# Second layer of a two-layer mixer on one core: keys projected in one load ahead of the last gate-input load, values in whole tiles behind the last queries, key norms earlier

## What is computed

```python
z = h @ o_w_in
c_u, c_v, cq, ckv, kr = split(z, [512, 1024, 1408, 1664])
yc = spatial_gating(gelu(c_u), gelu(c_v), w_s, bias, v_gain)
q  = (rmsnorm(cq) @ w_uq).reshape(s, 8, 96)
kv = (rmsnorm(ckv) @ w_ukv).reshape(s, 8, 128)
k_nope, v = kv[..., :64], kv[..., 64:]
q, k = rmsnorm per head and part, rope on 32 columns, shared rotary key joined to k_nope
yd = softmax(chunk-causal q k) v
y  = concat(rmsnorm(yc), rmsnorm(yd)) @ o_w_out
```

## Time and profile before

| | us |
|---|---|
| median of 3 runs (lowest, highest) | 1105.81 (1105.48, 1106.58) |
| the profiled execution, its own time | 1106.4 |
| its span, first to last instruction | 1104.6 |
| PE busy (matmuls) | 1096.0 (99%) |
| DVE busy | 548.3 (50%) |
| ACT busy | 418.3 (38%) |
| POOL busy | 104.4 (9%) |
| mean granted TensorE clock | 1.000 |

### The profile page before, as it was taken

One profiled execution on the slowest core, in us unless ns is written; L12 is line 12 of the kernel. 1 busy time (PEld: TensorE's weight loads), 2 busy tenths in 40 slices (PEclk: granted clock), 3 DMA queues, 4 the chain that ended last, 5 costly groups with the idle time before them and its releaser, 6 DMA issues. The chain is left out here.

```text
span 1104.6 us, 13734 instructions
## 1 busy us (share of the span) xinstructions
PE 1096.0 (99%) x5148; PEld 883.8 (80%) x5148; DVE 548.3 (50%) x770; ACT 418.3 (38%) x663; POOL 104.4 (9%) x126
## 2 busy tenths in 40 slices
PE   9999999999999999999999999999999999999998
PEld 7777788888888888888878766788888888888887
DVE  6677967344334433242466588655434433453321
ACT  5546435333223222131446557545223322332110
POOL 6000000010001000000102023000001100100000
PEclk9999999999999999999999999999999999999999
DMA  7522233332333333332233200233333233327431
GB/s 225 172 58 82 72 105 106 96 95 88 101 95 95 95 96 97 99 103 88 72 96 93 84 20 2 77 115 95 96 96 99 89 112 96 95 77 173 113 125 47
DMA packets 103241, 106.00 MB, mean 96 GB/s; under 512 B 26267, under 2 KB 79968, under 8 KB 103200
## 3 DMA queue, kind: packets, MB, share of 16 engines
q1 hardware_dynamic: 85488, 103.04, 30.6%
q10 hardware_dynamic: 16656, 2.10, 1.2%
q0 software_dynamic: 1056, 0.30, 0.1%
HBM read 101.23 MB, written 2.10 MB: 94 GB/s over the span
## 5 line engine op out<-in xcount | busy, mean ns | idle before, releaser
L1126 DVE TENSOR_TENSOR w_lo<-raw,w_hi 128x1024 fp32r<-128x1024 f32 (+2 forms) x192 | 224.6, 1176 | 420.7 <-ACT w_hi L700 417.9
L700 ACT ACTIVATE w_hi<-raw 128x1024 fp32r<-128x1024 f32 (+2 forms) x192 | 194.4, 1017 | 466.7 <-PE ps L1688 434.9
L1686 PE MATMUL ps<-h_hi,w_hi 128*128 128x512 f32 x912 | 359.7, 394 | 0.7 <-DVE h_lo L1150 0.7
L1687 PE MATMUL ps<-h_lo,w_hi 128*128 128x512 f32 x912 | 355.1, 389 | 0.0
L1688 PE MATMUL ps<-h_hi,w_lo 128*128 128x512 f32 x912 | 355.1, 389 | 0.0
L1686 PEld LDWEIGHTS ps<-h_hi,w_hi 128*128 128x128 f32 x912 | 171.3, 188 | 41.3 <-issue 5.6
L1687 PEld LDWEIGHTS ps<-h_lo,w_hi 128*128 128x128 f32 x912 | 171.3, 188 | 36.6 <-issue 1.7
L1688 PEld LDWEIGHTS ps<-h_hi,w_lo 128*128 128x128 f32 x912 | 171.2, 188 | 36.0
L584 POOL TENSOR_TENSOR ffn_t<-ffn_t,row_scale 128x512 f32<-128x512 f32 x40 | 50.9, 1294 | 606.9 <-ACT ffn_t L887 606.9
L1687 PE MATMUL ps<-w_lo,act_hi 128*128 128x512 f32 (+1 forms) x178 | 68.8, 387 | 0.0
L1688 PE MATMUL ps<-w_hi,act_lo 128*128 128x512 f32 (+1 forms) x178 | 68.8, 387 | 0.0
(11 more groups left out here) (288 smaller groups left out, 1151.7 us busy)
## 6 DMA issues: line engine op xcount, KB each, us to landing
raw<-in_w_ffn_in SPq DMA_DIRECT2D x88, 512.0 KB, 3.5
raw<-in_w_ffn_out SPq DMA_DIRECT2D x44, 512.0 KB, 3.9
raw<-in_e_w_in SPq DMA_DIRECT2D x17, 512.0 KB, 3.7
raw<-in_o_w_in SPq DMA_DIRECT2D x8, 512.0 KB, 3.6
raw<-in_o_w_out SPq DMA_DIRECT2D x8, 512.0 KB, 3.7
raw<-in_e_w_out SPq DMA_DIRECT2D x8, 256.0 KB, 3.9
raw<-in_e_w_out SPq DMA_DIRECT2D x4, 512.0 KB, 4.7
out_tok<-x_blocks ACTq DMA_DIRECT2D x16, 128.0 KB, 2.6
```

Source lines behind the costliest of these rows:

```text
L700: ins = act.activation(dst, src, ACT.Copy)
L1126: ins = TT(dst, src, high, ALU.subtract)
L1686: MM(dst, st_hi, mv_hi, start=start, stop=False)
L1687: MM(dst, st_hi, mv_lo, start=False, stop=False)
```

## The change

It renumbers the loads: 104, 105 queries, 106 to 108 c_u, 109 keys of all eight heads (`O_UK`), 110 last c_u load, 111, 112 queries, 113 values of all heads (`O_UV`). The loads 109 and 113 take 64 of every 128 columns of `w_ukv`, in two transfers each.

```diff
-O_CQ, O_CKV, O_CV, O_UKV, O_OUT = 92, 96, 100, 112, 114
-O_UQ, O_CU = (104, 105, 110, 111), (106, 107, 108, 109)
+O_CQ, O_CKV, O_CV, O_OUT = 92, 96, 100, 114
+O_UQ, O_CU, O_UK, O_UV = (104, 105, 111, 112), (106, 107, 108, 110), 109, 113
...
+            if n in (O_UK, O_UV):
+                free(n)
+                for k in range(2):
+                    sp.dma_start(raw[:, n % 2, 512 * k:512 * k + 512].rearrange("p (h c) -> p h c", h=HEADS),
+                                 w_ukv[:, k, :, 0 if n == O_UK else 1, :]).then_inc(raw_landed[n % 2], 16)
...
# ACT
         through(107)
+        through(108)
+        key_squares()
+        key_gains()
+        through(109)
+        rms(M_OK, ps[:, 4, :], 1)
         gelu_table()
-        through(109)
         for j in range(4):
             act.wait_ge(u_scaled, j + 1)
             act.activation(u_c[:, j, :], u_c[:, j, :], ACT.Gelu_apprx_tanh).then_inc(u_ready, 1)
-        q_squares(2, 4)
+        q_squares(2, 6)
         through(110)
         rms_table()
         q_squares(3, 6)
-        yc_square(0)
-        yc_square(1)
-        key_squares(0)
-        rms(M_OQ + 1, ps[:, 3, :], 1)
-        yc_square(2)
-        yc_square(3)
-        key_squares(1)
-        key_gains_1()
-        rms(M_OK, ps[:, 4, :], 1)
-        value_copy(0, 0, 0)
-        rms(M_OC, ps[:, 1, :], 512)
+        for j in range(4):
+            yc_square(j)
+        for t in range(QT):
+            value_copy(t)
+        rms(M_OQ_LATE, ps[:, 6, :], 1)
+        rms(M_OC, ps[:, 7, :], 512)
         exp_table()
...
# DVE
         through(108)
+        key_gains()
+        through(109)
         dve.wait_ge(load_used, O_CU[3] + 1)
         for j in range(4):
             TT(u_c[:, j, :], ps[:, j, :], row_scale[:, :], ALU.mult).then_inc(u_scaled, 1)
-        through(109)
-        q_tiles(2, 4)
+        rms(M_OK, ps[:, 4, :], 1)
         through(110)
+        q_tiles(2, 6)
+        k_norm(0)
+        k_norm(1)
...
-        yc_gate(0)
-        yc_gate(1)
+        for j in range(4):
+            yc_gate(j)
         q_tiles(3, 6)
-        yc_gate(2)
-        yc_gate(3)
-        key_gains_0()
-        rms(M_OQ + 1, ps[:, 3, :], 1)
-        yc_sum(1)
-        yc_sum(2)
-        q_scale(1, (0, 1, 2, 3))
-        rms(M_OK, ps[:, 4, :], 1)
-        yc_sum(3)
-        value_copy()
-        k_norm(0)
+        for j in range(1, 4):
+            yc_sum(j)
+        k_norm(2)
+        k_norm(3)
...
+        dve.wait_ge(ov_act, 3)
+        for i in range(QT):
+            set_mask(i)
+        rms(M_OQ_LATE, ps[:, 6, :], 1)
+        rms(M_OC, ps[:, 7, :], 512)
...
         o_max(0)
-        k_norm(2)
+        q_scale(1, (3, 6, 7, 4))
         o_prob(0)
         o_max(1)
         o_pt(0)
         o_prob(1)
         o_max(2)
-        k_norm(3)
...
# PE
         cu_load(2)
+        pe.wait_ge(ckv_lo_ready, 2)
+        pe.wait_ge(oq_scaled, 4)
+        load(O_UK, plain(512, 4), range(2), lambda k: (ckv_hi[:, k, :], ckv_lo[:, k, :]), range(4, 8), True, True)
         cu_load(3)
-        pe.wait_ge(oq_scaled, 2)
-        q_load(2, 4)
+        pe.wait_ge(ok_squared, 4)
+        pe.wait_ge(ok_gained_dve, 1)
+        sums4(4, [mean64[:, 48:80]] * 4, [q_sq(p) for p in range(4)])
+        pe.wait_ge(ok_gained, 2)
+        q_load(2, 6)
+        pe.wait_ge(ok_gained_dve, 2)
+        spread(M_OK, (4, 5))
         pe.wait_ge(u_scaled, 4)
         pe.wait_ge(cv_normed, 4)
...
-        pe.wait_ge(oq_scaled, 4)
+        pe.wait_ge(oq_turned, 6)
         q_load(3, 6)
...
+        ready(O_UV)
+        value_tile(0)
+        value_tile(1)
+        pe.wait_ge(ok_normed, 4)
+        spread(M_OK, (4, 5), 2)
+        value_tile(2)
+        value_tile(3)
+        q_sums(1, 6)
         pe.wait_ge(yc_summed, 4)
-        mean(M_OC, 1, ones, acc[:, :])
+        mean(M_OC, 7, ones, acc[:, :])
...
-                    pe.wait_ge(banks_set, (2, 5, 5, 5)[n])
+                    pe.wait_ge(banks_set, 4)
...
         o_scores(0)
-        pe.wait_ge(ov_act, 2)
-        value_tiles(1, 1, 3)
-        pe.wait_ge(ok_normed, 2)
+        pe.wait_ge(ov_act, 4)
+        pe.wait_ge(rs_step, M_OC + 1)
+        pe.wait_ge(ok_normed, 6)
+        spread(M_OQ_LATE, (3, 6, 7, 4))
         o_scores(1)
-        pe.wait_ge(ov_act, 3)
-        pe.wait_ge(ok_normed, 6)
+        pe.wait_ge(oq_scaled, 8)
+        pe.wait_ge(ok_normed, 8)
```

More of the change, by code:

```diff
@@ L101, in load_dmas @@
         return 3
+    if n in (O_UK, O_UV):
+        return 2
     return 1
@@ L507, in _ @@
             wide(O_CV + j, oin, 256 * j, 512, 512)
-        for n in range(O_UQ[0], O_UKV):
+        w_ukv = o_w_ukv[0].rearrange("(k p) (h two c) -> p k h two c", p=P, two=2, c=64)
+        for n in range(O_UQ[0], O_OUT):
             if n in O_CU:
                 wide(n, oin, 256 * O_CU.index(n), 0, 512)
+                continue
+            if n in (O_UK, O_UV):
+                free(n)
+                for k in range(2):
+                    sp.dma_start(raw[:, n % 2, 512 * k:512 * k + 512].rearrange("p (h c) -> p h c", h=HEADS),
+                                 w_ukv[:, k, :, 0 if n == O_UK else 1, :]).then_inc(raw_landed[n % 2], 16)
                 continue
@@ L712, in through, with spare_column @@
                 nxt[0] += 1
+        n_spare = [0]
+        def spare_column():
+            n_spare[0] += 1
+            return spare[:, n_spare[0] - 1:n_spare[0]]
         def exp_table():
-            act.activation(spare[:, :], eps_col[:, :], ACT.Exp)
+            act.activation(spare_column(), eps_col[:, :], ACT.Exp)
         def rms_table():
-            act.activation(spare[:, :], eps_col[:, :], ACT.Abs_reciprocal_sqrt)
+            act.activation(spare_column(), eps_col[:, :], ACT.Abs_reciprocal_sqrt)
         def h_high_first(ft):
@@ L980, in gelu_table, with key_squares, key_gains, value_copy @@
         def gelu_table():
[L982 to L996, removed]
-            else:
-                act.wait_ge(ov_tiles, half + 1)
-            act.activation(o_v[:, 2 * part:2 * part + 2, 256 * half:256 * half + 256],
-                           ps[:, bank, :].rearrange("p (t c) -> p t c", t=2), ACT.Copy).then_inc(ov_act, 1)
+            act.activation(spare_column(), eps_col[:, :], ACT.Gelu_apprx_tanh)
+        def key_squares():
+            act.wait_ge(load_used, O_UK + 1)
+            for p in range(4):
+                act.activation(q_sq(p), ps[:, 4 + p, :], ACT.Square).then_inc(ok_squared, 1)
+        def key_gains():
+            for p in (2, 3):
+                act.wait_ge(ok_squared, p + 1)
+                act.activation(k_pairs[:, p, :], ps[:, 4 + p, :], ACT.Copy, scale=g_col(G_OK)).then_inc(ok_gained, 1)
+        def value_copy(t):
+            if t == QT - 1:
+                act.wait_ge(load_used, O_UV + 1)
+            else:
+                act.wait_ge(ov_tiles, t + 1)
+            act.activation(o_v[:, t, :], ps[:, t, :], ACT.Copy).then_inc(ov_act, 1)
         def yc_square(j):
@@ L1725, in sums4, with spread @@
             ins.then_inc(sums_ready, 1)
-        def spread(m, banks):
+        def spread(m, banks, g0=0):
             pe.wait_ge(rs_ready, m + 1)
-            for g, b in enumerate(banks):
+            for g, b in enumerate(banks, g0):
                 ins = MM(ps[:, b, :], sel[32 * g:32 * g + 32, :], rs_of(m)[32 * g:32 * g + 32, :], start=True, stop=True)
@@ L2112, in value_tiles @@
[L2112 to L2137, removed]
@@ L2138, in _, with value_tile @@
-        spread(M_OK, (4, 5, 6, 7))
-        pe.wait_ge(oq_scaled, 6)
+        def value_tile(t):
+            pe.wait_ge(gates_ready, t + 1)
+            for kk in range(2):
+                c = slice(512 * kk, 512 * kk + 512)
+                ins = product(ps[:, t, :], ckv_hi[:, kk, t * P:(t + 1) * P], ckv_lo[:, kk, t * P:(t + 1) * P],
+                              w_hi[:, O_UV % W_SLOTS, c], w_lo[:, O_UV % W_SLOTS, c], kk == 0, kk == 1)
+            ins.then_inc(load_used if t == QT - 1 else ov_tiles, 1)
```

73 lines of the change are left out of this document (20 added, 53 removed).

## The result

The kernel with the change takes 1109.72 us (median of 6 runs, 1108.99 to 1110.03), the kernel before 1106.07 us beside it (6 runs, 1105.48 to 1106.58): +3.65 us, ratio 1.0030 with a 95% interval of 1.0019 to 1.0040. That is more than the 0.2% which the prediction took as the least that can be told from no change; the lower end of the interval lies about there. The profiled execution took 1108.99 us, its span is 1107.2 us.

The account below looks back on a forecast made before the run. PE is busy 99% overall, but DVE bounds the attention's start: first division 4.3 us later, 0.3 regained, net +4.0 on 1106.4 gives 1110.4 profiled, 1109.8 as median. Range 1106.5 to 1112.0.

Parts of the forecast that it names:

- ACT's rounding of load 114 ends: On ACT behind key scale, gelu table, gelus and query squares: ends at 640.4, 7.4 us later than before.
- DVE's wait for it: DVE, free at about 636.4, waits 4 us for ACT's rounding before load 114's low part; new with the change.
- masks: Four memsets on DVE ahead of the first scores, 2 x 0.18 us, done at 657.8.
- PE's wait for the masks: PE, through at about 655, waits 2.8 us until 657.8 ahead of head 0's scores.
- first division: DVE's division for head 0 in the attention: at 665.3 instead of 661.01, 4.3 us later.
- regained behind it: Steady attention: the fourth pair of key norms gone from behind head 2's maxima gives 0.3 of PE's 0.45 us waiting back.
- The hand-overs: Gaps between DVE's rows up to the first division: some 0.03 us each over a dozen groups, 0.4 us.
- half a spread: Part of PE's work after the values, with query sums and one mean, putting PE through at about 655.
- PE stays the bound: Rival: DVE reaches the masks by the time PE does, so first heads' waits mostly go; -1.6 us, 1104.2; 12%.
- Swallowed: Rival: DVE's later list is less dense than added up, so the delay shrinks to under 2 us; about 1107; 13%.
- Late key load: Rival: the key load's 256-byte runs land up to 7.2 us late, ahead of ACT's list; 3.5 on top, 1113; 5%.
- Clock: Rival: the pause of 2.8 us ahead of the first scores lowers PE's granted clock; about +2, 1112; 5%.

Follow-up runs that it names:

- e3: Changed kernel plus four unused multiplications in VectorE's dense list, behind the key norms of heads 0 to 3; 1112.71 us, ratio 1.0057 to before.
- e4: Changed kernel plus the same four unused multiplications in VectorE's idle time, ahead of the key gains; 1109.61 us, ratio 1.0033 to before.
- e1: Changed kernel with VectorE rounding load 114 behind the turning of query heads 4 and 5, not ahead; 1108.61 us, ratio 1.0018 to before.
- e2: Changed kernel with load 114 rounded late: ScalarE behind the table switch, VectorE behind head 2's maxima; 1108.45 us, ratio 1.0018 to before.
- e5: Changed kernel with the placement undone: last gate-input chunk ahead of the key load again, gates' mixing right behind it; 1109.94 us, ratio 1.0042 to before.
- e6: Changed kernel with query heads 4 to 7 each scaled singly behind the transposes of heads 1 to 4; 1113.09 us, ratio 1.0063 to before.
- e12: Against the run with placement undone, PE fed and ScalarE copying scales: key scales spread by four matmuls side by side, not two pairs; 1106.23 us.
- e9: Changed kernel with both the placement undone (e5) and the query scaling done singly (e6); 1114.53 us, ratio 1.0077 to before.
- e8: Changed kernel with both load 114 rounded late (e2) and the query scaling done singly (e6); 1110.78 us, ratio 1.0043 to before.

## Why the prediction was right

The time, 1109.72, lies 0.1 from the forecast of 1109.8. In part that is luck: the change cost 0.35 less than the 4.0 forecast, and the kernel before, in six runs, stood 0.26 above the median of three that the forecast started from. On the axis of before (after's times + 1.07):

| step of the prediction | predicted | measured |
|---|---|---|
| ACT's rounding of load 114 ends | 640.4 | 640.25 |
| DVE's wait for it | 4 | 4.16 |
| masks | 657.4 to 657.8 | 657.10 to 657.43 |
| PE's wait for the masks | 2.8 | 1.44 |
| first division | 665.3 (+4.3) | 664.57 (+3.56) |
| regained behind it | 0.3 | -0.16 |
| net | +4.0 | +3.65 (median), +3.72 (projection) |

**The chain held**: key scale, table, gelus and load 114 on ACT, DVE's wait, its dense list, masks, division. e3 and e4 show that the list was on the path, e1 and e2 that load 114's place cost 1.4 to 1.6 us. One sign that the prediction named did not come: PE was to wait over 2 us for a mask, and waited 1.44.

**Three sizes were off.** The hand-overs: I added 0.4 us for gaps, but many neighbours on DVE overlap. The low part lasts 1.22 and the queries start 1.14 behind its start; these last 1.40 and the norms start 1.32 behind. Others, such as the rms steps, stand 0.04 apart. From low part to division it is 24.22 us, where I had 24.9. The regained 0.3: nothing came back; PE is busy 21.61 of 22 us in the steady attention, as before, so taking the fourth pair of key norms away from there gained nothing. These two errors cancelled in part. And PE's wait for the masks: I counted "half a spread" for the second pair of key scales, but it takes as long as a whole one (1.13). PE was through at 656.14 on the axis of before, where I had about 655, and the masks came a little sooner; so PE waited less. The end didn't depend on it.

**The rivals.** *PE stays the bound*: no, PE waits for DVE; when the list was shortened (e2), PE's order became the next bound once the division had come 1.66 us earlier. *Swallowed*: no, the 3.56 us at the division are 3.72 at the projection. *Late key load*: no. The transfers view (KB, median us to landing) and ACT's rounding of load 109, which waits for nothing and on the axis of before starts at 603.55, as there:

```profile
raw<-in_o_w_ukv SPq DMA_DIRECT2D x4, 256.0 KB, 3.4
```

```profile
602.48 1.06 ACT L701 ACTIVATE w_hi<-raw 128x1024 fp32r<-128x1024 f32 x1
```

*Clock*: 1.00 in after's windows, in spite of the wait of 1.44. But a lower clock does occur in this kernel's variants: e5 shows it right behind a wait of 1.71.

## What to carry to other kernels

When an order changes, read what it does to the engine that the bound waits for: 2.87 us of work there was free in one gap and cost 2.9 us further down its list. An operation that nobody needs soon (here a weight's low part, due 55 us on) should not stand ahead of a dense list when it waits for another engine. Before moving small matmuls apart, see whether they run side by side, and when a variant misses its time, look at the granted clock of its executions first.

## What the runs showed that I had not expected

Four 32-row spreads take 1.14 us together, two 1.13, one 1.12: splitting them multiplies their price (e6, e12). And the clock's answer to a wait is not told by its length: it fell behind 1.71 us in e5 (0.92 and 0.74 in the windows), in two of five executions by their mean clock, and in all five of e9, but stayed at 1.00 in the windows of e3 around waits of 2.12 and 1.94 us. In e9's trace it fell a second time (0.93 and 0.73 from 660 to 670), behind waits of only 0.40 and 1.13. Nor is one trace the whole: one or two executions of e1, e2, e4 and e8 and two of e3's five, none of them profiled, have a mean of 0.998. What makes the difference these runs don't settle.
